# Two norms of a hybrid decoder step: two modulation panels loaded ahead of the second weight panel, one of them taken ahead of the sum of squares and the last behind the walk

## The reference, cut to what matters

```
mod = silu(c) @ w_ada + b_ada                       # 9 vectors of 2048: shift, scale and gate of three parts
h = h + 0.5 * gt1 * swiglu(modulate(h, g1, sh1, sc1), w_ffn1_up, w_ffn1_down)
xm = rmsnorm(h, g_mix) * (1 + scm) + shm            # first seam: norm 1
proj = xm @ w_in                                    # 24 column panels of q, k, v first
h = h + gtm * (merged @ w_out)
x2 = rmsnorm(h, g_ffn2) * (1 + sc2) + sh2           # second seam: norm 2
h = h + 0.5 * gt2 * swiglu(x2, w_ffn2_up, w_ffn2_down)
```

## Time and profile before

| | us |
|---|---|
| median of 3 runs | 2687.14 |
| lowest, highest | 2687.06, 2688.66 |
| the profiled execution | 2686.34 |
| its span in the trace | 2684.5 |
| PE busy in it | 2628.0 |
| mean granted PE clock, of full speed | 0.993 |

### The profile page before, as it was taken

How to read it: one execution, slowest core, us unless ns; L and a number is a source line. 1 busy time by engine, 2 the same in 40 slices (tenths; PEclk the granted TensorE clock), 3 DMA queues, 4 the chain that set the end, 5 groups by cost and what they waited for, 6 DMA issues and landing times.

```text
span 2684.5 us, 49412 instructions
## 1 busy us (share of the span) xinstructions
PE 2628.0 (98%) x21449; PEld 2472.4 (92%) x21449; DVE 1409.7 (53%) x1795; ACT 1053.3 (39%) x1086; POOL 22.5 (1%) x49
## 2 busy tenths in 40 slices
PE   7999999999999999999999999999999999999998
PEld 4889999999999789999989999899899999999997
DVE  3554455444455766655556554375644455444455
ACT  4343333333344433644424444343433333333443
POOL 0000000000000000000010000000000000000000
PEclk9999999999999999999999999999999999999999
DMA  9987755677755887433377565777666655545453
GB/s 398 381 316 265 257 186 191 248 255 264 253 188 187 290 311 274 141 126 111 110 276 266 217 218 206 276 255 270 235 209 232 212 186 191 194 175 185 152 189 129
DMA packets 130576, 605.58 MB, mean 226 GB/s; under 512 B 10464, under 2 KB 10720, under 8 KB 84336
## 3 DMA queue, kind: packets, MB, share of 16 engines
q1 hardware_dynamic: 125584, 582.06, 60.4%
q0 software_dynamic: 4256, 20.59, 2.0%
q10 hardware_dynamic: 576, 0.56, 0.1%
HBM read 590.55 MB, written 12.62 MB: 225 GB/s over the span
## 4 chain that ended last, share of the span: by engine, by line
PE 90%; DVE 4%; DMA 3%; ACT 2%; issue 1%; SPq 0%; DVEq 0%; ACTq 0%; POOLq 0%
PE acc L2101 47%; PE acc L2109 23%; PE acc L2392 4%; PE mp L2190 4%; PE acc L2397 2%; PE acc L2279 2%; DMA raw<-in_ada 2%; DVE wlo L1362 1%; PE mp L2086 1%; ACT whi L889 1%; PE acc L2304 1%; PE mp L2458 1%; PE mp L2463 1%; DMA h<-in_x 0%; PE mp L2168 0%
## 5 line engine op out<-in xcount | busy, mean ns | idle before, releaser
L1362 DVE TENSOR_TENSOR wlo<-raw,whi 128x2048 fp32r<-128x2048 f32 (+2 forms) x427 | 888.7, 2081 | 737.7 <-ACT whi L889 735.2
L889 ACT ACTIVATE whi<-raw 128x2048 fp32r<-128x2048 f32 (+2 forms) x427 | 743.8, 1742 | 495.3 <-PE acc L2109 391.1
L2101 PEld LDWEIGHTS acc<-xhi,whi 128*128 128x128 f32 x3808 | 477.0, 189 | 47.2 <-issue 46.3
L2101 PE MATMUL acc<-xhi,whi 128*128 128x264 f32 x3808 | 509.6, 287 | 1.1 <-ACT whi L889 0.6
L2101 PE MATMUL acc<-xlo,whi 128*128 128x264 f32 x3808 | 499.0, 284 | 0.0
L2109 PE MATMUL acc<-xhi,wlo 128*128 128x264 f32 x3808 | 498.5, 284 | 0.0
L2101 PEld LDWEIGHTS acc<-xlo,whi 128*128 128x128 f32 x3808 | 476.2, 188 | 0.0
L2109 PEld LDWEIGHTS acc<-xhi,wlo 128*128 128x128 f32 x3808 | 475.7, 188 | 0.0
L2109 PE MATMUL acc<-uhi,wlo 128*128 128x264 f32 x1408 | 191.7, 284 | 0.0
L2101 PE MATMUL acc<-uhi,whi 128*128 128x264 f32 x1408 | 190.7, 283 | 0.0
L2101 PE MATMUL acc<-ulo,whi 128*128 128x264 f32 x1408 | 190.1, 283 | 0.0
(11 more groups left out here) (388 smaller groups left out, 1954.2 us busy)
## 6 DMA issues: line engine op xcount, KB each, us to landing
raw<-in_up SPq DMA_DIRECT2D x160, 1024.0 KB, 4.8
raw<-in_ada SPq DMA_DIRECT2D x144, 1024.0 KB, 7.9
raw<-in_down SPq DMA_DIRECT2D x128, 704.0 KB, 4.0
raw<-in_win SPq DMA_DIRECT2D x69, 1024.0 KB, 6.4
raw<-in_wgate SPq DMA_DIRECT2D x32, 1024.0 KB, 4.8
blk<-in_up SPq DMA_DIRECT2D x16, 1024.0 KB, 7.8
raw<-in_wout SPq DMA_DIRECT2D x16, 1024.0 KB, 5.0
raw<-in_wproj SPq DMA_DIRECT2D x24, 512.0 KB, 4.8
```

The lines of the kernel that those rows point to most:

```text
L889: act.activation(whi[:, s.slot(SPLIT), 0:width], raw[:, r.slot(RAW), 0:width], ACT.Copy)\
L1362: v.tensor_tensor(wlo[:, s.slot(SPLIT), 0:width], raw[:, r.slot(RAW), 0:width], whi[:, s.slot(SPLIT), 0:width].bitcast(F32), ALU.subtract)\
L2101: mm(dst, whi[:, b, (tile + k) * P:(tile + k + 1) * P], x[part], start=starts and part == 0 and k == 0, stop=False)
```

## The change

- In the ring, panel 1 moves from entry 2 to entry 4. The modulation panels then are entries 2, 3, 5 and 6. The entries from 7 on are as before.
- PE takes modulation panel 0 ahead of `total_squares`, panels 1 and 2 between that and the walk, and panel 3 behind the walk, ahead of the low matmuls of panel 1.
- DVE's `split_lo` of panel 1 moves from behind the norm's fourth tile to behind its last.
- ACT's order stands, but its `split_hi` of panel 1, still between `root` and the norm, now waits for entry 4.

```diff
 PARK = 2
-LO_AHEAD = 3
+SEAM_PANEL, SEAM_ADA = (0, 1, 4), (2, 3, 5, 6)
...
                     if early is not None and k <= PARK:
-                        load(At(r0 - 4 + k), w[w0 + (k + PARK) % (PARK + 1)])
-                        if k == PARK:
-                            for q in range(4):
-                                load_ada(At(r0 - 1 + q), early[0], q)
+                        at = r0 - 4 + SEAM_PANEL[k]
+                        load(At(at), w[w0 + (k + PARK) % (PARK + 1)])
+                        if k:
+                            for q in range(2):
+                                load_ada(At(at + 1 + q), early[0], 2 * k - 2 + q)
...
-                        split_hi(At(S_QKV + 1), At(R_QKV + 2))
+                        split_hi(At(S_QKV + 1), At(R_QKV + SEAM_PANEL[2]))
...
-                    if k == LO_AHEAD:
-                        split_lo(s, r)
+                split_lo(s, r)
...
                 def begun():
-                    for m in range(3):
-                        ada(m, g, At(r + 3 + m))
-                    trio(At(s0), At(r), At(a0), ready, n, range(0, 10))
-                    ada(3, g, At(r + 6))
-                    trio(At(s0), At(r), At(a0), ready, n, range(10, KD))
+                    for m in range(1, 3):
+                        ada(m, g, At(r + SEAM_ADA[m]))
+                    trio(At(s0), At(r), At(a0), ready, n)
+                    ada(3, g, At(r + SEAM_ADA[3]))
+                    trio_low(At(s0 + 1), At(r + SEAM_PANEL[2]), At(a0 + 1))
                     fold(g)
...
                 if o:
+                    if n == 0:
+                        ada(0, G_N1, At(R_QKV + SEAM_ADA[0]))
                     total_squares(sq, sacc, 3 if n else 1)
...
             panels(OUT_BODY, S_OUT, R_OUT, A_OUT, G_OUT, 0, first_out)
+            ada(0, G_N2, At(R_FF2 + SEAM_ADA[0]))
             total_squares(sqo, sacco, 2)
```

More of the change, by code:

```diff
@@ L1346, in _ @@
             root(6)
-            split_hi(At(S_FF2 + 1), At(R_FF2 + 2))
+            split_hi(At(S_FF2 + 1), At(R_FF2 + SEAM_PANEL[2]))
             norm(2, SH2, G_N2, R_N2)
@@ L1633, in _ @@
                     FF1_PLANS[o], G_FIRST + o * G_FF1_HALF, False, GT1, FF1_BEGIN[o])
-            norm(1, SHM, SCM, At(S_QKV + 1), At(R_QKV + 2))
+            norm(1, SHM, SCM, At(S_QKV + 1), At(R_QKV + SEAM_PANEL[2]))
             take_ada(G_N1)
@@ L2068, in _ @@
             dve.wait_ge(h_tile, T_OUT + KD)
-            norm(2, SH2, SC2, At(S_FF2 + 1), At(R_FF2 + 2))
+            norm(2, SH2, SC2, At(S_FF2 + 1), At(R_FF2 + SEAM_PANEL[2]))
             take_ada(G_N2)
@@ L2112, in panel, with trio @@
                 last.then_inc(panel_used, 1)
-            def trio(s, r, a, ready, n, ks):
+            def trio(s, r, a, ready, n):
                 last = s + 1
[L2117 to L2123, removed]
+                for j in range(PARK + 1):
+                    fresh(a + j)
+                pe.wait_ge(park_hi_done, n)
+                pe.wait_ge(slot_done[r.slot(RAW)], (r.turn(RAW) + 1).val())
+                pe.wait_ge(hi_done, (last + 1).val())
+                pe.wait_ge(slot_done[(r + 1).slot(RAW)], ((r + 1).turn(RAW) + 1).val())
                 b, c = s.slot(SPLIT), last.slot(SPLIT)
-                for k in ks:
+                for k in range(KD):
                     xh, xl = xs[k]
@@ L2137, in trio, with trio_low @@
                     mm(to(a + 1), whi[:, c, w], xl, start=False, stop=False)
[L2138 to L2142, removed]
+            def trio_low(s, r, a):
+                c = s.slot(SPLIT)
+                pe.wait_ge(slot_done[r.slot(RAW)], (r.turn(RAW) + 1).val())
+                for k in range(KD):
+                    ins = mm(to(a), wlo[:, c, k * P:(k + 1) * P], xs[k][0], start=False, stop=k == KD - 1)
+                ins.then_inc(panel_used, 1)
             def walk(s, r, a, made, ready):
```

## The result

The changed kernel takes 2692.77 us in the median of 15 runs (2690.87 to 2699.16), the kernel before beside it 2687.1 (15 runs, 2683.4 to 2690.6). The medians are 5.7 us apart. The ratio is 1.0027, with a 95% interval of 1.002 to 1.0034: 5.4 to 9.1 us slower. The profiled execution took 2694.22 us with a span of 2692.4.

The account below looks back on a forecast made before the run. PE, busy 98% of the span, was taken as the bound, losing time only by waits or half clock. 4.2 + 2.3 - 0.4 = +6.1 us on 2686.34 gave 2692.4, with the median 0.8 above, 2693.3; range 2688.5 to 2696.5.

Parts of the forecast that it names:

- Part 1: Gap at the sum of squares, both norms: one modulation panel, 1.0 us, fits in; cost and gain nothing.
- Part 2: ACT ahead of norm 1: panel 1 lands at 889.3, norm delayed 0.4 us; no delay at norm 2.
- Part 3: Norm 1, behind the walk: late split holds entries 8 and 9, which meet the spill; +4.2 us (+1.1 to +6.3).
- Part 4: Norm 1, behind the walk: PE's clock falls to half in the wait; +2.3 us (0 to 2.9).
- Part 5: Norm 2, behind the walk: last modulation panel covers ACT's split of panel 3; -0.4 us (-0.6 to 0).
- A: Behind norm 1's walk: PE waits as said, but the clock holds; +3.8 us, 2690.9; chance 0.13.
- C: Behind norm 1's walk: two modulation panels go ahead of the spill, clock holds; +0.7 us, 2687.8; chance 0.10.
- E: Both seams: gain over 0.2%, below 2681.8, by an earlier walk, held clock and entries 8, 9 in time; chance 0.02.
- D: Norm 1: panel 1 lands at 890.6 or later, norm ends 1.3 us later; +8.0 us, 2695.1; chance 0.10.
- B: DMA behind norm 1's walk: q0 and q1 share evenly, entry 9 lands at 920.0; +4.7 us, 2691.8; chance 0.15.
- The rule of the Trainium skill: DMA queues: an engine takes turns between queues with work, a packet (bundle of descriptors) at a time; weighed against a trace row.
- the 0.62 us: PE's one wait between 895.0 and 931.96 at norm 1 in the kernel before, for entry 13.

Follow-up runs that it names:

- e2: Changed kernel with norm 1 as before, so the change at norm 2 alone: 2686.31 against 2687.28 for the kernel before, ratio 0.9995.
- e6: Kernel before, but at norm 1 PE takes entry 5's modulation panel in the walk after four tiles: 2686.36 against 2686.21, ratio 1.0001.
- e10: Kernel before, with the spill and stc held until entry 31 is taken: 2683.77 against 2685.98, ratio 0.9987.
- e4: Changed kernel, but POOL's spill waits until PE has taken entry 9's modulation panel: 2693.18 against 2687.28 for the kernel before, ratio 1.0022.

## Why the prediction was right

By its own steps, the seam of the changed kernel brought to the old clock (less 0.57 us):

- **Part 1** (one panel ahead of the squares, free): right at norm 1. The gap at the squares was filled, and the walk began 0.2 us later. At norm 2 the walk was to wait for the norm; it waited 2.78 us for entry 5's load and began 0.9 us later, counted from the squares.
- **Part 2** (panel 1 late, norm 0.4 us later): right in kind, the size 0.7 for 0.4. Panel 1 was there at 889.7, not 889.3. At norm 2, where no delay was expected, ACT waited 0.40 us for it.
- **Part 3** (+4.2): measured +5.0. The norm's end 906.5 for 906.1, the issue of entries 8 and 9 at 908.8 for 908.4, entry 9's landing 922.2 for 921.4. The landing is this near in part by luck, since one term was wrong and others made up for it. The spill's first bytes are in the trace 1.1 us after its issue (908.5, issued 907.40) and not 3.8 us; the engines were idle. It landed in 8.0 us where it had taken 12.1. But q1 moved nothing up to 914, where 0.3 MB by 916.2 had been allowed for, and ran at 281 GB/s from there to entry 9's start, below the 343 of the earlier trace rows; 2.47 MB went through q1 in that time, so part of them were entry 10's.
- **Part 4** (+2.3): the fall came, from 919.6 to 926.4 in the trace's own time. From entry 9's start to panel 5 it took 16.3 us (922.82 to 939.11) for 14.8 at full clock: 1.5 us. The forecast was 0.8 us too high here and 0.8 too low in part 3, and the sum did not feel it.
- **Part 5** (-0.4): -0.6 at norm 2, near the forecast but partly by another way. The walk began 0.9 us later; less of it ran at half clock (1.3 us, where it had been 3.4), which gave about as much back. How much of the 0.6 is the cover of ACT's split, I can't separate. That the late split does no harm there was right: no load behind the walk was waited for.
- Sum at norm 1 +6.6 against +6.5, at norm 2 -0.6 against -0.4. The profiled spans differ by 7.9 us; the other 1.9 lie outside the seams, and the medians, 5.7 apart, don't have them.

Of the rivals, A (clock holds) fell with the trace, C and E with the result. D fell with the trace too: panel 1 was there at 889.7, not 890.6, though the norm's end came 0.4 us behind the forecast, a third of D's 1.3. B is not told from the forecast by the time (2691.8), but by the trace: the windows from 909 to 914 show the spill alone in the engines with two modulation panels waiting. The rule of the Trainium skill that was weighed there (page "DMA: Bandwidth & Descriptors", section "Queues, rings and completion order") speaks of turns by packets. What the profile counts as a packet is of very unlike size in the two queues here (0.27 MB in 16 packets against 0.41 MB in 200). If these are the page's packets, unequal shares don't contradict it; no row says that they are. That q1 moved nothing for some us is not explained by it either way.

What the prediction had wrong did not show in its number: part 4 counted the half clock at norm 1 before as 2.9 us lost, and its reading of the stretch behind the walk took the 0.62 us for all that the loads cost there. In the kernel before neither held, because of the backlog: with the clock at full in the walk (e2) panel 5 started no earlier. In the changed kernel PE waits for entry 9 whatever its walk did, so the slip cost nothing here; it cost the forecasts of e6 and e10.

## What to carry to other kernels

When a buffer's release moves, ask which load is queued behind it, and what else will be on the DMA engines at that time: the order of the ring and of PE was free here, and one line, the place of the release, held back 2 MB of loads and cost about 6 us. A short wait in front of a load is not the measure of what the loads cost: if PE was slow ahead of it, the rest is hidden, and a gain ahead of it can be taken back, as it was twice here. A store that can wait, as the spill could for some 85 us, is better kept out of the one stretch where the loads are short; here that alone gave 1 to 6 us.

## What the runs showed of the hardware

- A 2.1 MB store from SBUF took the DMA engines nearly for itself: no q1 bytes from 909 to 914 in the changed kernel, with 2 MB of q1's loads issued at 909 to 911. With the spill held back (e4) the same loads' first bytes came about a us after their issue at 909.45.
- The same store landed 12.1 us after its issue where loads were ahead of it (before), and 8.0 us after it on idle engines (changed).
- The granted clock at norm 1 of the same code fell in one execution and held in another (0.58 against 1.00 in the window 893:900 of the kernel before and of the kernel with only norm 2 changed), with waits of PE that differ by under a us.
